# Gate projection of the second layer's attention stage as Strassen pairs of column chunks

## What is computed

```python
def _odd_mixer(h, hc, w_in, q_norm, k_norm, w_out, pos, need_ctx):
    ...
    def branch(p, attn):
        return (attn * jax.nn.silu(p[..., o_v:])) @ w_out
    p = h @ w_in
    k_l, v_l = kv_of(p[..., o_q:o_v], pos)
    ...
    y = branch(p, _attend(q_of(p[..., :o_q], pos), k, v))
```

## Time and profile before

| | |
|---|---|
| median of 3 runs | 3846.35 us (3840.49 to 3850.64) |
| the profiled execution | 3845.68 us, of which the span from first to last instruction is 3843.9 |
| PE busy | 3588.7 us, 93% of the span |
| DVE, ACT busy | 2000.7 us (52%), 684.7 us (18%) |
| mean granted TensorE clock | 0.98 of full speed |
| stage `att_c` | 1543.3 to 1741.9 us of the span |

### The profile page before, as it was taken

One profiled execution on the slowest core, in us unless ns is written; L12 is line 12 of the kernel. 1 busy time (PEld: TensorE's weight loads), 2 busy tenths in 40 slices (PEclk: granted clock), 3 DMA queues, 4 the chain that ended last, 5 costly groups with the idle time before them and its releaser, 6 DMA issues. The chain is left out here.

```text
span 3843.9 us, 60078 instructions
## 1 busy us (share of the span) xinstructions
PE 3588.7 (93%) x24845; PEld 1835.6 (48%) x24845; DVE 2000.7 (52%) x3216; ACT 684.7 (18%) x1371; POOL 561.7 (15%) x801
## 2 busy tenths in 40 slices
PE   8799998899989999999999999898998889989998
PEld 1354443334544446454444444453346666665443
DVE  0399994433346767236646657336533434334435
ACT  0100000121320112231100000325632222221000
POOL 0011111121100001000000010531212323322100
PEclk9899999999999999999999999999999999999999
DMA  8778996784235566425567586647863333335662
GB/s 298 282 280 306 352 374 240 282 323 148 81 141 197 197 215 226 133 88 219 208 213 252 201 309 231 222 150 269 277 192 120 116 114 106 107 104 177 226 233 109
DMA packets 362559, 799.05 MB, mean 208 GB/s; under 512 B 26574, under 2 KB 73702, under 8 KB 357674
## 3 DMA queue, kind: packets, MB, share of 16 engines
q1 hardware_dynamic: 259920, 459.69, 35.0%
q0 software_dynamic: 72736, 274.10, 19.7%
q10 hardware_dynamic: 29634, 61.45, 4.2%
HBM read 686.94 MB, written 108.22 MB: 207 GB/s over the span
## 5 line engine op out<-in xcount | busy, mean ns | idle before, releaser
L1444 PE MATMUL gemm_a_g_ps<-store_w,turned 128*128 128x512 f32 (+1 forms) x1152 | 455.1, 557 | 2.4 <-PEq L205 2.4
L975 DVE SCALAR_TENSOR_TENSOR pmods_acc<-pmods_w,cond,pmods_acc 128x512 f32<-128x512 f32 x540 | 384.5, 749 | 24.3 <-issue 1.3
L1444 PEld LDWEIGHTS gemm_a_g_ps<-store_w,turned 128*128 128x128 f32 x1152 | 208.4, 190 | 248.5 <-issue 248.5
L3173 PE MATMUL scan_g_ps<-store_w,turned 64*64 64x512 f32 x2048 | 295.6, 616 | 14.8 <-DVE outlet_stage L3187 6.9
L1444 PE MATMUL att_a_g_ps<-store_w,turned 128*128 128x512 f32 x512 | 240.2, 599 | 7.0 <-ACT outlet_stage L2921 4.2
L1444 PE MATMUL feat_g_ps<-store_w,turned 128*128 128x512 f32 x384 | 180.4, 618 | 15.9 <-ACT outlet_stage L2456 13.7
L1491 PE MATMUL out_c_g_ps<-store_w,turned 128*128 128x512 f32 x384 | 167.6, 592 | 0.0
L1444 PE MATMUL tail_g_ps<-store_w,tail_branch_t 128*128 128x512 f32 x384 | 165.7, 592 | 0.9 <-ACT tail_branch_t L4002 0.9
L3538 DVE TENSOR_TENSOR scan_tm<-scan_tm,scan_ps 128x256 f32<-128x256 f32 x128 | 53.9, 422 | 171.3 <-PE scan_ps L3426 171.0
L1444 PE MATMUL att_c_g_ps<-store_w,turned_c 128*128 128x512 f32 x256 | 128.2, 602 | 13.4 <-PEq L4077 13.4
L1444 PEld LDWEIGHTS att_a_g_ps<-store_w,turned 128*128 128x128 f32 x512 | 91.5, 191 | 100.1 <-issue 93.5
(11 more groups left out here) (534 smaller groups left out, 5907.7 us busy)
## 6 DMA issues: line engine op xcount, KB each, us to landing
store_w<-in_w_in SPq DMA_DIRECT2D x160, 1024.0 KB, 7.7
pmods_w<-in_w_mod POOLq DMA_DIRECT2D x40, 2048.0 KB, 12.1
store_w<-in_a_w_in SPq DMA_DIRECT2D x48, 1024.0 KB, 12.1
store_w<-in_c_w_in SPq DMA_DIRECT2D x40, 1024.0 KB, 7.9
mods_w<-in_w_mod SPq DMA_DIRECT2D x32, 1024.0 KB, 9.4
store_w<-in_a_w_out SPq DMA_DIRECT2D x32, 1024.0 KB, 5.7
scan_raw<-s_feat SPq DMA_DIRECT2D x112, 256.0 KB, 4.5
s_feat<-feat_o POOLq DMA_DIRECT2D x16, 1536.0 KB, 7.4
```

Source lines behind the costliest of these rows:

```text
L975: v.scalar_tensor_tensor(a, src, x, a, ALU.mult, ALU.add)
L1444: mm = pe.matmul(to, lhs, self.store.slot[i % self.store.NS][:, k, :width], start=first, stop=last)
L3173: mm = pe.matmul(self.ps[r][halves[o], :], self.act_tile(k, tb)[halves[r], halves[o]], self.store.slot[i % self.store.NS][halves[r], k % 4 ...
```

## The change

The four gate chunks become two pairs. The stage's 128 units become 2 x 7 x 8 = 112, and `order` is spread anew over them with the same rule. The lists of DVE and ACT get the pair's steps at marked unit counts: with U = 8 units per product and B = 0 or 56 units before the pair, the pieces x = 0..3 of form 1 stand behind unit B+2x, of form 2 behind B+8+2(x+1), of form 3 behind B+24+2x, of form 4 behind B+32+2x; u2 and u4 behind B+24, y01 behind B+32, u3 and y11 behind B+40, y00 behind B+48, y10 behind B+56. Silu now reads and writes SBUF (`result`), three units behind its sum. The forms lie in `rows_t[:, 3, :]` and a new buffer, the second pair's results in `rows_t[:, 2, :]`. The inputs are `turned_c` and the block sums in `turned`, which are there already. The gates are still multiplied one tile at a time, in the order in which the sums finish.

```diff
-        g = Ring(nc, st, f"{name}_g", store, [(w, tbs, act_tile) for w, tbs, func, dst in projections], 4)
-        out_of = outlet.take(0 if plan.gated else sum(len(tbs) for w, tbs, func, dst in projections))
+        upper_form = sb("upper_form", [P, KD // 4, NCH]) if inputs and plan.gated else None
+
+        def form_places(n):
+
+            return [rows_t[:, 3, :].rearrange("p (k c) -> p k c", c=NCH), upper_form]
+        g = Ring(nc, st, f"{name}_g", store, [(w, tbs, inputs.tile, inputs.wait) if inputs else (w, tbs, act_tile)
+                                              for w, tbs, func, dst in projections], 4, form_places if inputs and plan.gated else None)
+        out_of = outlet.take(0 if plan.gated else sum(4 if inputs else len(tbs) for w, tbs, func, dst in projections))
         prob, prob_t = [sb(f"prob{s}", [P, NCH]) for s in range(2)], [sb(f"prob_t{s}", [P, NCH]) for s in range(2)]
         ost = [] if plan.gated else [sb(f"ost{s}", [P, dv]) for s in range(4)]
         stat = sb("stat", [P, 4, 4])
+        results = [x[:, :] for x in outlet.stage] + [rows_t[:, 2, n * NCH:(n + 1) * NCH] for n in range(4 if inputs and plan.gated else 0)]
...
+        job_units = [7 * g.product_units(n) if inputs else len(job[1]) * KD for n, job in enumerate(g.jobs)]
+        order, left = [], sum(job_units)
...
-        dve_order, done, ripe = [], 0, []
+        result_of = {"y00": (0, 0, 0), "y11": (1, 1, 1), "y01": (2, 0, 1), "y10": (3, 1, 0)}
+        dve_at, act_at = {}, {}
...
+        for n in range(len(g.jobs) if inputs else 0):
+            U, B, pieces = g.product_units(n), sum(job_units[:n]), store.pieces(g.base + n)
+            spread = ([(B + U * x // pieces, ("T", n, 1, x)) for x in range(pieces)]
+                      + [(B + U + U * (x + 1) // pieces, ("T", n, 2, x)) for x in range(pieces)]
+                      + [(B + 3 * U + U * x // pieces, ("T", n, 3, x)) for x in range(pieces)]
+                      + [(B + 4 * U + U * x // pieces, ("T", n, 4, x)) for x in range(pieces)])
+            for at, item in (spread
+                             + [(B + 3 * U, ("u", n)), (B + 4 * U, ("sum", "y01", n)),
+                                (B + 5 * U, ("sum", "y11", n)), (B + 6 * U, ("sum", "y00", n))]):
+                dve_at.setdefault(at, []).append(item)
+            for at, item in ((B + U, ("snap", n, 1)), (B + 2 * U, ("snap", n, 5)), (B + 4 * U + 3, ("result", "y01", n)),
+                             (B + 5 * U + 3, ("result", "y11", n)), (B + 6 * U + 3, ("result", "y00", n))):
+                act_at.setdefault(at, []).append(item)
...
+        for n in range(len(g.jobs) if inputs else 0):
+            end = sum(job_units[:n + 1])
+            dve_at.setdefault(end, []).append(("sum", "y10", n))
+            act_at.setdefault(min(end + 3, sum(job_units)), []).append(("result", "y10", n))
+
+        dve_order, done, ripe = list(dve_at.get(0, [])), 0, []
...
         for item in order:
             if item[0] == "unit":
                 done += 1
-                ripe += [t for t in range(len(g.tiles)) if plan.gated and g.finished_by(t) == done]
+                dve_order += dve_at.get(done, [])
+                if plan.gated:
+                    ripe += [t for t in range(len(g.tiles)) if g.finished_by(t) == done]
+                    ripe += [item[1:] for item in dve_at.get(done, []) if item[0] == "sum"]
             elif item[0] in ("turn", "score", "value", "rowturn"):
                 dve_order.append(item)
             for t in list(ripe):
-                n, j = g.tiles[t]
-                last = plan.last_unit(n, projections[n][1][j])
-                if (last is None or ("value", last) in dve_order) and done >= g.finished_by(t) + 6 and t == ripe[0]:
+                last = plan.last_unit(*place_of(t))
+                if (last is None or ("value", last) in dve_order) and done >= finished(t) + 6 and t == ripe[0]:
                     dve_order.append(("gate", t))
                     ripe.remove(t)
         dve_order += [("gate", t) for t in ripe]
+        gates = [item[1] for item in dve_order if item[0] == "gate"]
+        if inputs:
...
+            for item in order:
+                if item[0] == "unit":
+                    done += 1
+                    act_order += act_at.get(done, [])
+                else:
+                    act_order.append(item)
+        made = [item[1:] for item in act_order if item[0] == "result"]
...
                 for n in range(len(g.jobs)):
+                    if inputs:
+                        yield from g.pair_units(pe, n, None)
+                        continue
...
+            def upper(n):
+                p1, p5, u4, u3 = slots(n)
+                if plan.gated and n == 0:
...
+                g.sum_u2(v, n, 0, p1, u3)
...
+                g.sum_u4(v, n, 0, u3, p5, u4)
+
+            def sum_(what, n):
+                p1, p5, u4, u3 = slots(n)
+                if what == "y01":
+                    g.sum_y01(v, n, 0, u4)
+                elif what == "y11":
+                    g.sum_u3(v, n, 0, u3)
+                    g.sum_y11(v, n, 0, u3, p5)
+                elif what == "y00":
+                    g.sum_y00(v, n, 0, p1)
+                else:
+                    g.sum_y10(v, n, 0, u3)
+
+            def gate_result(key):
...
+                v.wait_ge(copied, made.index(key) + 1)
+                v.drain()
+                a = rows_t[:, tb, chunk * NCH:(chunk + 1) * NCH]
+                v.tensor_tensor(a, a, slots(n)[result_of[what][0]], ALU.mult).then_inc(gated, 1)
...
+            forms = {}
             for item in dve_order:
-                if item[0] == "turn":
+                if item[0] == "T":
+                    n, form = item[1:3]
+                    if len(item) == 4:
+                        if item[3] == 0:
+                            forms[n] = g.make_form(v, n, form)
+                        next(forms[n])
...
+                elif item[0] == "u":
+                    upper(item[1])
+                elif item[0] == "sum":
+                    sum_(*item[1:])
...
+            def result(what, n):
...
+                g.wait_added(act, n, what, 0)
+                act.activation(results[4 * n + x], results[4 * n + x], func).then_inc(copied, 1)
...
@@ -4149,12 +4276,12 @@
...
-        c_gate = c_chunks(LAT, C_GATE, C_END, ACT.Silu)
...
+        c_gate = in_pairs(c_chunks(LAT, C_GATE, C_END, ACT.Silu))
...
-        attend_and_project(nc, "att_c", store, outlet, ident, GroupedPlan(proj_c, rows_t, tiled), 128 ** -0.5, 128, xc, c_gate, 16, 0,
-                           rows_t=rows_t)
+        attend_and_project(nc, "att_c", store, outlet, ident, GroupedPlan(proj_c, rows_t, tiled), 128 ** -0.5, 128, None, c_gate, 16, 0,
+                           rows_t=rows_t, inputs=PairInputs(nc, None, turned_c[:, :], turned[:, :], KD, 512, (0,), (1,), (0,), (1,)))
```

More of the change, by code:

```diff
@@ L2692, in load_count @@
             return 16 * sum(len(plan.loads(x)) for x in range(n % plan.slots, n + 1, plan.slots))
-        order, left = [], sum(len(tbs) for w, tbs, func, dst in projections) * KD
+        job_units = [7 * g.product_units(n) if inputs else len(job[1]) * KD for n, job in enumerate(g.jobs)]
+        order, left = [], sum(job_units)
         def fill(count):
@@ L2740, in attend_and_project, with finished, place_of @@
                 act_order.append(item)
-        dve_order, done, ripe = [], 0, []
+        result_of = {"y00": (0, 0, 0), "y11": (1, 1, 1), "y01": (2, 0, 1), "y10": (3, 1, 0)}
[18 more added lines that the diff above has]
+        dve_order, done, ripe = list(dve_at.get(0, [])), 0, []
+        def finished(key):
+            return g.finished_by(key) if not inputs else sum(job_units[:key[1]]) + 8 * (PAIR_ORDER.index(int({"y01": 3, "y11": 7, "y00": 2, "y10": 4}[key[0]])) + 1)
+        def place_of(key):
+            if not inputs:
+                n, j = g.tiles[key]
+                return n, projections[n][1][j]
+            what, n = key
+            return 2 * n + result_of[what][2], result_of[what][1]
         for item in order:
```

35 lines of the change are left out of this document (34 added, 1 removed).

## The result

| | before | after |
|---|---|---|
| median of the runs | 3846.35 us (3840.49 to 3850.64) | 3824.45 us (3819.46 to 3836.55) |
| span of the profiled execution | 3843.9 us | 3819.7 us |
| `att_c`, from its first unit to the first product of `out_c` | 209.5 us | 198.3 us |
| the scan, a later stage | 664.1 us | 651.8 us |

The changed kernel takes 0.9942 of the time of the kernel before, 95% interval 0.9927 to 0.9958: 21.9 us less, where I forecast 9.9 less.

The account below looks back on a forecast made before the run. PE bounds the stage. 3845.68 - 13.1 (units removed) + 2.8 (stalls) + 0.8 (end) - 0.4 (start of `out_c`) = 3835.8 us, or 3836.4 against the median, 9.9 less; range 3830 to 3844, chance 0.62.

Parts of the forecast that it names:

- Removal: In `att_c`, 128 units become 112: seven fourth units at 0.77 us and nine third ones at 0.86 save 13.1 us.
- Stalls: DVE's added work overflows its idle holes and delays PE by 2.8 us, walked mark by mark; bounds 0.5 and 9 us.
- mark 80: A piece and u2, u4 in the hole ahead of the reciprocal, in a two-unit round, make PE 1.4 us late.
- 24 to 26: A piece and u2, u4 ahead of the maximum, then a piece ahead of the reciprocal: 0.4 us on PE.
- 61 and 62: Three gates and a piece make the maximum 2.2 us late, but the next hole is empty: 0 on PE.
- the eight pieces there: Forms 1 and 2 of the first pair, in the 16 units ahead of the softmax, cost nothing.
- The added sum: At the end of `att_c`, a DVE sum between the last unit and Silu adds 0.8 us.
- the start of `out_c`: PE's wait for copies shortens as weight loads finish earlier: 0.4 us won, between 0 and 0.9.
- Rival 3: A piece holds DVE for about 2.2 us: stalls of 14 us in `att_c`, 3847.7 us in all, chance 0.04.
- Rivals 2 and 4: 2: DVE often late, stalls 9 us, 3842.7 us, chance 0.14. 4: PE pays all DVE sums, 3872 us, chance 0.05.
- Rival 1: Nothing overflows: stalls 0.5 us, start of `out_c` wins 0.9, 12.7 us less, 3833.7 us, chance 0.15.
- the sum against the profiled execution: All terms, from `att_c` and the start of `out_c`, applied to the whole 3845.68 us, giving 3835.8 us.

Follow-up runs that it names:

- marks: The changed kernel with five marks of DVE's added steps moved by one to three units: 3820.7 us, `att_c` 195.8 us; repeated, 3824.0 us and 196.2 us.
- double: The changed kernel with a DVE reduction of 128x1024 put ahead of each of the 32 pieces of forms: 3838.6 us, `att_c` 211.2 us.
- after_w112: The changed kernel with 112 already met waits added to TensorE's list at the end of `out_a`: 3840.1 us, 0.9981 of the kernel before.
- before_again: The kernel before, unchanged, run again: 3848.7 us, 1.0007 of the kernel before in the same batch.

## Why the prediction was half right

**What bounds the stage** was right: with 16 units fewer PE stays the bound, 161.3 of 165.0 us.

**Removal.** I took 13.1 and named 13.7 as the other end. From the first unit to the end of the last matmul the stage takes 185.8 us, 197.1 before: 11.3 less. The rounds bear out 13.1: 5.78 us with four units, 5.01 with three, 4.15 or 4.16 with two, so 0.77 and 0.86 us a unit, as I had taken. marks, in which PE waits for no scaling, takes 183.6 us, 13.5 less than the kernel before. That is the 13.1 and 0.4 that I had not counted: the kernel before lost 0.37 us in its first step, where PE waited for the scaling, and the changed kernel does not:

```profile
1570.07 1.10 PE L2796 MATMUL att_c_sc<-att_c_kt,att_c_qt 128*128 128x512 f32 x2 [0.29 <-DVE rows_t L2875]
```

**Stalls.** 2.8 forecast, 2.1 measured, the difference of marks and the changed kernel over the same stretch. By the distances of value product and score it is 1.08 at mark 80 (1.4 forecast), 0.32 at 88 (0.6), 0.21 at 72 (0.3), 0 at 24 to 26 (0.4), 0 at 61 and 62: 1.6 in the steps. What I had not walked through is the lead: the first group's copies stand behind the last piece of form 2, and its transposes waited 1.10 us, 0.35 before. Of these 0.75 us more, 0.5 were left at the first step, which makes 2.1 in all. The prediction said that the eight pieces there cost nothing because PE needs them late; true for the products, but not for the copies behind them in DVE's list. marks moved that piece too, and the wait went. double tells that the walk gives the size at twice the load too, though in part by luck: 12.9 us more, 11.2 by the walk, with the 3.7 of the transposes not in it.

**Ends.** The added sum cost 0.64 (0.8 forecast), the start of `out_c` won 0.52 (0.4), for the reason given: ACT's issue no longer meets full queues, and DVE's copy behind form 1 is what PE waits for. By the sum, 13.1 + 0.4 - 2.1 - 0.64 + 0.52 = 11.3 us; the difference of the stage is 11.2.

**Rivals.** Rival 3 falls by the rows: a piece ahead of a PSUM read holds DVE for 1.14 us. The Trainium skill's rule of a drain nearly as long as the operation ("VectorE: DVE Perf Modes", "The DRAIN you can't avoid") doesn't show in these rows either, now with a PSUM sum or a reduction behind the piece. The section itself says that a next operation which isn't held starts earlier, so it is no contradiction; my prediction had left that sentence out. Rivals 2 and 4 fall by the waits of 1.2 us. Rival 1 (12.7 us) is 1.5 above the stage's 11.2 and the forecast (9.9) 1.3 below it, so by size alone the two can hardly be told apart. By mechanism it is the forecast: the waits came at the marks of the walk, each somewhat shorter than it gave. Of rival 1's two reasons, the wider hole behind a late step may be why they were shorter, which is not shown; 0.86 us for a fourth unit is wrong.

**The step that failed** is the sum against the profiled execution: it took 9.9 us off the whole, as if the other 3650 us could not change. No term stood for them, and the sum gave no reason why. They fell by another 8.5 to 11.1 us in the three comparisons of the last column. after_w112 shows what the forecast was about: with the borders of TensorE's blocks put back, the change gives 9.4 us (3 to 12 by its interval). That this is so close to 9.9 is partly luck, as the stage alone gives 11. The rest is no work that the change saves: it comes from TensorE's list being 56 instructions shorter, and from where the kernel before happened to have its borders. Five kernels with place 0 or -2 lie between -3.9 and +3.2 us of the kernel before in the last column; fourteen runs with five other places lie between -18.8 and -8.5. Over the profiles, with the first one of before added to the five, the scan takes 661.9 us on the mean at the old place and 651.7 at the others. Half of that is idle time of PE (74.9 and 69.8 us), most of it time that nothing in the profile releases (42.1 and 37.8 us). The other half is PE's busy time (587.0 and 581.9); the lower clock, which held for 26.1 and 19.1 us, can make some 3.5 of these 5.1 us, by my estimate from half the difference of these two.

**What stays open.** Not each border pauses: of some 126 in the scan 13 to 17 do, and which ones depends on the place. Those that pause are those whose packet started late, 217 of 294 times behind a border at which the DMA engines were full of other loads; no run shows that these loads are the cause. Nor is it shown why the places 0 and -2 are bad and -22, +14, +28, +33 and +79 are not: they differ more in the length of the pauses (12.5 of a scan are over 1.5 us at the old place, 9.1 at the others, on the mean) than in their number. Differences among the others are within the spread. A single profile can mislead here too: the scan of one kernel, before, took 664.1 and 655.1 us in two executions, and the second belongs to the fastest of the 12 executions of before_again, 15 us below their median.

## What to carry to other kernels

Walk through the list of the engine that is to take on the work, hole by hole, with measured lengths, and include what stands behind the added steps in its list, the lead of the stage too: this gave 11.2 us to within 1.3. Then look for stages with thousands of short matmuls that come later: an edit ahead of them that changes the length of TensorE's list moves the borders of its instruction blocks, and here that was worth some 12 us, as much as the change. To tell the two apart, add met waits where TensorE is idle until the pauses stand where they stood.

## What the runs showed of the hardware that I had not expected

- TensorE's instruction queue moved one packet of 16.4 KB per 256 instructions (127 matmuls with their weight loads, and waits); in the scan, one in 5.2 us. At 13 to 17 borders of a scan TensorE stood for 1.0 to 3.6 us, mostly at the same ones in each execution of a kernel, and went on 2.2 to 2.9 us after the start of a packet. A row at the lower clock followed such a pause (0.50 in 2964.2 to 2967.6, busy throughout).
- Met waits are not free: 512 of them at one place are 256 instructions in the trace, moved the list by one whole block, and made TensorE's idle time ahead of `att_c` 25.0 us, where it had been 13.4.
- A matmul stage whose own work is left alone can still differ between builds: 651.7 us on the mean at five places of the borders, 661.9 at the old one, for the same 16,096 matmuls. Single profiles ran from 645.2 to 666.3 us, and those of one kernel differed by 9 us.
